# A gated delta rule laid out anew in a three-block kernel, with head norms and expert one-hots in other forms

## What is computed

```python
decay = exp(where(incl, gc[:, None] - gc[None, :], -inf))        # gc: running sum of g in the chunk
kk = einsum('id,jd->ij', k * beta, k) * decay
a_mat = eye + where(strict, kk, 0)
u, w = solve(a_mat, v * beta), solve(a_mat, k * beta * exp(gc))
attn = einsum('id,jd->ij', q, k) * decay
def step(state):                                                   # over the chunks
    v_new = u - w @ state
    o = (q * exp(gc)) @ state + attn @ v_new
    state = state * exp(g_last) + (k * exp(g_last - gc)).T @ v_new
```

## Time and profile before

| | us |
|---|---|
| median of 3 runs | 4513.59 |
| lowest and highest | 4506.96, 4524.67 |
| the profiled execution | 4514.63 |
| its span in the profile | 4512.9 |

### The profile page before, as it was taken

One profiled execution on the slowest core, in us unless ns is written; L12 is line 12 of the kernel. 1 busy time (PEld: TensorE's weight loads), 2 busy tenths in 40 slices (PEclk: granted clock), 3 DMA queues, 4 the chain that ended last, 5 costly groups with the idle time before them and its releaser, 6 DMA issues. The chain is left out here.

```text
span 4512.9 us, 50869 instructions
## 1 busy us (share of the span) xinstructions
PE 3787.8 (84%) x18835; PEld 3223.6 (71%) x18835; DVE 2688.0 (60%) x3850; ACT 1178.9 (26%) x1989; POOL 562.7 (12%) x381
## 2 busy tenths in 40 slices
PE   7998966799976556799899998999968877679998
PEld 6876753588755346579889898999946837556876
DVE  4444777444345565439999967777743447564433
ACT  1101123211031201113377773333321112322300
POOL 0000021000000020001456662222200000000000
PEclk9999978899988868899999999999979988889999
DMA  3222700222212000225888789999912102011232
GB/s 139 98 72 83 271 15 1 100 93 74 77 38 83 0 6 1 89 76 183 290 271 284 281 303 325 329 328 322 319 53 89 56 21 75 2 65 62 96 98 70
DMA packets 198406, 590.97 MB, mean 131 GB/s; under 512 B 22336, under 2 KB 80704, under 8 KB 196040
## 3 DMA queue, kind: packets, MB, share of 16 engines
q1 hardware_dynamic: 161368, 454.46, 29.2%
q0 software_dynamic: 36864, 134.23, 8.4%
HBM read 536.19 MB, written 52.43 MB: 130 GB/s over the span
## 5 line engine op out<-in xcount | busy, mean ns | idle before, releaser
L332 DVE CAST w_hi<-w_ring 128x1024 fp32r<-128x1024 f32 (+1 forms) x336 | 238.6, 710 | 642.4 <-PE banks L297 493.7
L71 DVE TENSOR_TENSOR w_lo<-w_ring,w_hi 128x1024 fp32r<-128x1024 f32 (+1 forms) x336 | 424.6, 1264 | 11.5
L297 PE MATMUL banks<-x_hi,w_hi 128*128 128x512 f32 x896 | 355.8, 397 | 48.2 <-DVE x_lo L71 47.4
L1803 PE MATMUL up_ps<-h_hi,u_hi 128*128 128x384 f32 x1024 | 358.5, 350 | 35.8 <-DVE u_lo L71 35.6
L2083 PE MATMUL out_ps<-w_hi,v_hi 128*128 128x384 f32 x1024 | 346.8, 339 | 42.3 <-DVE w_lo L71 42.3
L297 PE MATMUL banks<-x_lo,w_hi 128*128 128x512 f32 x896 | 354.1, 395 | 0.0
L297 PE MATMUL banks<-x_hi,w_lo 128*128 128x512 f32 x896 | 353.9, 395 | 0.0
L1803 PE MATMUL up_ps<-h_lo,u_hi 128*128 128x384 f32 x1024 | 349.3, 341 | 0.0
L1803 PE MATMUL up_ps<-h_hi,u_lo 128*128 128x384 f32 x1024 | 348.8, 341 | 0.0
L2083 PE MATMUL out_ps<-w_hi,v_lo 128*128 128x384 f32 x1024 | 345.4, 337 | 0.0
L2083 PE MATMUL out_ps<-w_lo,v_hi 128*128 128x384 f32 x1024 | 345.3, 337 | 0.0
(11 more groups left out here) (495 smaller groups left out, 8113.5 us busy)
## 6 DMA issues: line engine op xcount, KB each, us to landing
expert_tiles<-peer_u SPq DMA_DIRECT2D x128, 512.0 KB
expert_tiles<-peer_v SPq DMA_DIRECT2D x128, 512.0 KB
w_ring<-w_in SPq DMA_DIRECT2D x104, 512.0 KB, 3.7
w_ring<-ffn_up SPq DMA_DIRECT2D x88, 512.0 KB, 3.4
w_ring<-w_ff SPq DMA_DIRECT2D x64, 512.0 KB, 3.7
ada_ring<-w_ada SPq DMA_DIRECT2D x48, 512.0 KB, 5.4
peer_acts<-act_ring SPq DMA_DIRECT2D x128, 192.0 KB
peer_gates<-staging SPq DMA_DIRECT2D x12, 2048.0 KB, 11.1
```

The lines of the kernel that those rows point to most:

```text
L71: return nc.vector.tensor_tensor(self.lo[at], value, self.hi[at].bitcast(F32), ALU.subtract)
L297: last = nc.tensor.matmul(banks[:, j, s, 0:n], a[:, u % 2, k, :], b[:, g * kg + k, x_from + c:x_from + c + n], start=(g == 0 and k == 0 an ...
L332: nc.vector.tensor_copy(w_parts.hi[:, u % 2], ring[:, u % slots]).then_inc(hi_ready, 1)
L1803: last = nc.tensor.matmul(up_ps[:, n % 3, 0:DENSE], a[:, n % 2, k, :], b[:, k, P:T], start=(k == 0 and part_ == 0), stop=(k == DB - 1 and ...
```

## The change

1. **Head norms.** `head_norm` now uses `HeadColumns`: the sums of squares come from matmuls with the squares as weights and one column of ones (tokens on partitions, 4 per tile), so root and reciprocal act on 128x16 or 128x32; ScalarE then draws diagonals (128x128, 4 per tile) that TensorE spreads over all partitions, and VectorE reads them from PSUM. The norm in `hgrn_and_conv` uses `HeadRows`: sums of the 4 heads on 4 partitions, one root and one reciprocal of 4x512, spread by 4 matmuls with 4 weight rows.
2. **Step sizes.** `delta_steps` is one block in place of the projection of a and b, the tables, the norm of q and k, softplus, sums: a and b come out as 128x8 per chunk of tokens (32 matmuls of 8 columns), the softplus runs on 128x16, and the compensated sums stay on 4x512 rows, with the scaling of q and k between them.
3. **Distances.** `delta_products` forms a chunk's whole distance in one matmul of stacked high and low sums (`left`, `own`), ScalarE takes Relu and Exp, and v and k are turned in the same block. Nothing is loaded.
4. **Inverse.** `delta_inverse` sets the first level directly (a mask and a transpose), runs five levels in full and half of the last, and uses the waits for growing q and k.
5. **Chain.** `delta_chain` forms the part of the values that does not depend on the state, and the weights WT of the state, ahead; a chunk's step is then a product with the state added in PSUM, a copy by ScalarE (which scales by beta), and the state's update.
6. **Loads.** The tables of the block-2 mixer are fetched behind the first weight tiles of its first `linear`; the two `load` blocks there and the two in the delta rule are gone.
7. **Experts.** 96 candidates of 256 are kept per head, the two products of hits and indices move from GpSimd to VectorE, the first one-hot is one fused compare-and-multiply per token (4 of 128x128 per group in place of one 128x512 on each of two engines), GpSimd keeps only the gathers, and the table of costs and phases has other numbers (tiles 14, 9, 32, 27, 25, 19 in place of 16, 9, 27, 26, 26, 22).

ScalarE at the head of the delta rule, before: squares of q and k (`sq`), roots (`rstd`), the sigmoid of beta (`rows`), `small` the exponent of a_log, and the softplus' two steps.

All 8 products of hits and all 96 of gates have left its queue. The diff, cut to its core:

```diff
+class HeadColumns:
...
+    def sum(self, pe, b, square):
+        for c in range(NC):
+            last = self.p.nc.tensor.matmul(self.sums[:, b, c:c + 1], square[:, c * P:c * P + P], self.p.ones[:, 0:1],
+                                           start=True, stop=True)
+        last.then_inc(self.summed, 1)
...
+    def draw(self, act, b):
+        if b == 0:
+            act.wait_ge(self.inverted, 1)
+        if b >= 2:
+            act.wait_ge(self.spread, b - 1)
+        for c in range(NC):
+            last = self.p.nc.scalar.activation(self.diag[:, b % 2, c, :], self.p.ident, ACT.Copy, scale=self.cols[:, b, c:c + 1])
+        last.then_inc(self.drawn, 1)
+    def spread_to(self, pe, b, bank):
+        pe.wait_ge(self.drawn, b + 1)
+        for c in range(NC):
+            last = self.p.nc.tensor.matmul(bank[:, c * P:c * P + P], self.p.ones, self.diag[:, b % 2, c, :],
+                                           start=True, stop=True)
+        last.then_inc(self.spread, 1)
...
+class HeadRows:
...
+    def sum(self, pe, b, square):
...
+        self.p.nc.tensor.matmul(self.sums[:], self.strip[:, self.nb - 1 - b:2 * self.nb - 1 - b], square,
+                                start=(b == 0), stop=(b == self.nb - 1)).then_inc(self.summed, 1)
...
+    def spread_to(self, pe, b, bank):
+        pe.wait_ge(self.inverted, 1)
+        self.p.nc.tensor.matmul(bank, self.sel[:, b, :], self.root, start=True, stop=True).then_inc(self.spread, 1)
...
-                    nc.vector.reciprocal(rms[:, sl], rms[:, sl]).then_inc(normed, 1)
...
+                    dve.wait_ge(norm_rows.spread, h + 1)
...
-                nc.vector.reciprocal(rstd[:, g, :], rstd[:, g, :]).then_inc(inverted, 1)
...
+def delta_steps(p, h, w_ab, small, qkv, beta, left, right, head_mask, grown, decayed):
...
+            for b in range(NB):
+                pe.wait_ge(sq_ready, b + 1)
+                norm_.sum(pe, b, sq[:, b, :])
+            for b in range(NB):
+                if b == 1:
+                    pe.wait_ge(g_ready, 1)
+                    for c in range(NC):
+                        last = nc.tensor.transpose(row_ps[:, c * P:c * P + P], g[:, c, :], p.ident)
+                    last.then_inc(rows_turned, 1)
+                if b >= 4:
+                    pe.wait_ge(scaled, b - 3)
+                norm_.spread_to(pe, b, banks[:, b % 4, :])
...
+            scale(1)
+            dve.wait_ge(row_taken, 1)
...
+            then(nc.vector.tensor_tensor_scan(hi, keep[:], g_row[:], 0.0, ALU.mult, ALU.add))
...
+            scale(2)
...
+            scale(3)
+            then(nc.vector.tensor_tensor(err, hi, lo[:], ALU.subtract))
+            then(nc.vector.tensor_tensor(err, prev, err, ALU.subtract))
...
-                        nc.tensor.matmul(bank_a[:, h, :], sel[:, h, :], rows[:, 1, :], start=True, stop=True) \
-                            .then_inc(spread, 1)
...
+            def distance(j):
+                pe.wait_ge(own_ready, j + 1)
+                if j >= 2:
+                    pe.wait_ge(floored, j - 1)
+                for c in range(NC):
+                    last = nc.tensor.matmul(dist_ps[:, j % 2, c, :], left[:, at(c)], own[:, j % 2, at(c)], start=True, stop=True)
+                last.then_inc(dist_done, 1)
...
+                nc.scalar.activation(tile, dist_ps[:, j % 2], ACT.Relu, scale=-1.0).then_inc(floored, 1)
+                act.wait_ge(floored, j + 1)
+                nc.scalar.activation(tile, tile, ACT.Exp, scale=-1.0).then_inc(decay_ready, 1)
...
+def delta_inverse(p, masks, qkv, col, N, XT, k_rows, k_grown):
...
+            for l in range(1, LEVELS):
+                n = l - 1
+                pe.wait_ge(level_ready, l)
+                for j in range(H):
+                    pe.wait_ge(begun, 2 * H)
+                    if n:
+                        pe.wait_ge(updated, 2 * H * (n - 1) + 2 * j + 2)
+                    for c in range(NC):
+                        i = j * NC + c
+                        columns = slice(0, HALF) if l == LAST else slice(0, P)
+                        last = nc.tensor.matmul(bank_a[:, j, c, columns], N_l[:, l % 2, i, :], X[:, i, columns], start=True, stop=True)
+                    last.then_inc(y_ready, 1)
+                for j in range(H):
+                    pe.wait_ge(y_taken, H * n + j + 1)
+                    if n == 0:
+                        pe.wait_ge(q_grown, j + 1)
+                    for c in range(NC):
+                        i = j * NC + c
+                        if l == LAST:
+                            last = nc.tensor.matmul(bank_b[0:HALF, j, c, 0:HALF], Y[:, i, 0:HALF], XT[:, i, HALF:], start=True, stop=True)
+                            continue
+                        nc.tensor.matmul(bank_b[:, j, c, :], Y[:, i, :], XT[:, i, :], start=True, stop=True)
+                        last = nc.tensor.matmul(bank_a[:, j, c, :], XT[:, i, :], Y[:, i, :], start=True, stop=True)
+                    last.then_inc(z_ready, 1)
...
+def delta_chain(p, qkv, beta, through, attn, v_rows, k_rows, k_grown, XT, o):
...
+            def outputs(c):
+                pe.wait_ge(w_taken, NC - 1)
+                if c >= 2:
+                    pe.wait_ge(o_taken, c - 1)
...
+                for j in range(H):
+                    bank = o_ps[:, c % 2, j, :]
+                    last = nc.tensor.matmul(bank, vn[:, c % 2, j, :], attn[:, j * NC + c, :], start=True, stop=(c == 0))
+                    if c:
+                        last = nc.tensor.matmul(bank, S[:, (c - 1) % 2, j, :], q[:, j, c * P:c * P + P], start=False, stop=True)
...
+            own_values(0)
+            state_weights(1)
+            carry(0)
+            own_values(1)
+            state_weights(2)
+            values(1)
+            state_weights(3)
+            outputs(0)
+            carry(1)
+            values(2)
+            outputs(1)
+            carry(2)
+            values(3)
+            outputs(2)
+            outputs(3)
...
-    MIDDLE = [2.6] + [0.85] * 4 + [1.0] * 8 + [0.85] * 4 + [1.0] * 4 + [3.9]
-    COSTS = {"route": HEAD + MIDDLE + [4.6, 2.3, 1.1], "gate": [0.72] * GROUPS, "dot": [1.3] * SLOTS}
+    MIDDLE = [1.8] + [0.5] * 4 + [0.65] * 8 + [0.5] * 4 + [0.65] * 4 + [4.2]
+    COSTS = {"route": HEAD + MIDDLE + [2.3, 4.6, 2.3, 2.3, 1.1], "gate": [1.15] * GROUPS, "dot": [1.3] * SLOTS}
...
-            def hits(c, j):
-                pool.wait_ge(hit_made, 2 * c + j + 1)
-                i2 = idx_f[:].rearrange("p (h two) k -> p h two k", two=2)
...
-            def weights(g):
-                c, at = g // GROUPS + 1, g % GROUPS * GROUP_TOKENS
-                pool.wait_ge(row_ready, g + 1)
-                nc.gpsimd.tensor_tensor(gated[:, g % HOTS], gated[:, g % HOTS],
-                                        over(picks[:, c % 2, 2, at:at + GROUP_TOKENS].unsqueeze(2), [P, GROUP_TOKENS, NKEYS]),
-                                        ALU.mult).then_inc(weights_ready, 1)
...
+                for at, first, rows, width in ((0, 0, 2, K), (32, 2, 2, 8), (48, 4, 12, 4)):
+                    shape = [P, H, rows, width]
+                    then(nc.vector.tensor_tensor(
+                        cand[:, :, at:at + rows * width].rearrange("p h (a b) -> p h a b", a=rows),
+                        over(v2[:, :, 0, first:first + rows].unsqueeze(3), shape),
+                        over(v2[:, :, 1, 0:width].unsqueeze(2), shape), ALU.add))
...
+                i2 = idx_f[:].rearrange("p (h two) k -> p h two k", two=2)[:, :, 1, :]
+                flat = hit[:].rearrange("p h k a -> p (h k) a")
+                for j, (marks, relation, table) in enumerate(((row_start[:], ALU.is_ge, row_diff[:]), (iota[:, 0:K], ALU.is_equal, i2))):
+                    then(nc.vector.tensor_tensor(flat, over(part_f[:, j].rearrange("p h k -> p (h k)").unsqueeze(2), [P, H * K, K]),
+                                                 over(marks.unsqueeze(1), [P, H * K, K]), relation))
                     yield
...
+                    settled()
+                    then(nc.vector.tensor_tensor(hit[:], hit[:], over(table.unsqueeze(2), [P, H, K, K]), ALU.mult))
+                    yield
+                    settled()
+                    then(nc.vector.tensor_reduce(token[:, j, :], flat, AX.X, ALU.add))
...
-                nc.vector.tensor_tensor(gated[:, g % HOTS], over(iota[:].unsqueeze(1), shape),
-                                        over(picks[:, c % 2, 0, at:at + GROUP_TOKENS].unsqueeze(2), shape), ALU.is_equal) \
-                    .then_inc(row_ready, 1)
+                for t in range(at, at + GROUP_TOKENS):
+                    nc.vector.tensor_scalar(gated[:, g % HOTS, t - at, :], iota[:], picks[:, c % 2, 0, t:t + 1],
+                                            picks[:, c % 2, 2, t:t + 1], ALU.is_equal, ALU.mult).then_inc(weights_ready, 1)
...
-        head_norm(p, o, dst, gain, o, H, 1, out=dst)
+        head_norm(p, o, dst, gain, dst, H)
```

1097 lines of the change are left out of this document (613 added, 484 removed).

## The result

| | before | after |
|---|---|---|
| median, us | 4517.24 (4 runs) | 4333.45 (4 runs) |
| lowest and highest | 4506.96, 4524.67 | 4323.88, 4340.69 |
| span of the profiled execution | 4512.9 | 4338.9 |

The ratio is 0.9593, with a 95% interval from 0.9566 to 0.9621: 184 us less, where 189 were forecast. The profiled execution after is the slowest of its four; its span is 174.0 us shorter than the one before.

What follows compares the result with a forecast made beforehand. Bounds: a serial delta-rule stage (294 us) whose engines mostly wait for one another, and the experts' first half, with at most 64 us to give. Terms 118 + 7 + 15 + 7 + 42 = 189 off 4514.6 give 4325, range 4275 to 4390.

Steps and rivals of the forecast that it cites:

- Steps: Delta rule's first block, from z through the scaling of q and k: 44 us against 86.4, bounds 36 and 50.
- Products: Delta rule's products of k, distances and turns: 80 at 0.21 us plus start and copies, 23 us against 46.
- Inverse: Delta rule's inverse: 8.5 us of VectorE start, five levels of 10.7, half level 6.5; 69 us against 90.
- Chain: Delta rule's four chunks, with part of the values formed ahead: 23 us against 47, bounds 19 and 34.
- Norm: Norm at the delta rule's end, behind the chunks: 17 us against 23, bounds 14 and 19.
- block 1: Block 1's norm: three of four reciprocals go, four-row products come; 7 us less, bounds 4 to 10.
- retention: Retention's norm, 44 us with 27 in reciprocals: 15 us less, bounds 10 to 20.
- Experts: Experts' first half, 692 us: lifting GpSimd's hold on VectorE and evening the phases gives 42 us less, bounds 0 and 60.
- A, the clock stays low: Delta rule: narrow products and idle gaps keep TensorE's clock low; 35 us less gain, retention 5; time 4365, chance 0.17.
- B, the experts' half gives nothing: Experts' first half: fused operations hold up GpSimd's gathers, VectorE waits for rows; the 42 us vanish, 4367, chance 0.15.
- C, the floor: Experts' first half reaches TensorE's floor, another 18 to 22 us, and delta-rule lower bounds 11 more: 4292, chance 0.2.
- D: Kernel slower: the experts' fused operation costs far more than its nearest row, 0.74 us each undoing 189 us; chance 0.02.

## Why the prediction was right, and where it was not

The time (4333 against 4325) and the signs of all terms were right. By its own steps:

- **What bounds.** The three views were enough: the reading that the first part and the chain count steps, the inverse counts matmuls, and that the experts' half can give no more than 64 us held. It gave 51, by the mean of eight profiles.
- **Steps, 44 forecast, 46.6 measured.** The 64 products ahead of the root took 10.6 + 13.8 = 24.4 us against 22; the forecast that narrow products lower the clock was right, at 0.67 and then 0.50. The widening shows that it was the width here: with 128 columns in both places the clock stayed at 1.00. The prediction took that from the earlier trace rows without proof.
- **Products, 23 forecast, 18.6 measured.** Mis-sized on the safe side, and in the turns. The start at half clock did take place: TensorE had no work for 6.37 us before the block, then ran at 0.50 for 4.1 us and at 0.87 for 4 more, at the price of some 2.5 us (an estimate: those two stretches at 1.00 would have taken 2.0 and 3.5), where I had put 3. But I had put the 32 turns at 0.21 us each, the price of a product. A turn stands as one record and takes half of that, 0.11 us (the group behind the eight of the last row begins 0.87 us after them), 3.5 us in all in place of 6.7; the statement ahead of the prediction that a plain f32 matmul has two rows doesn't hold for them. TensorE's first group, and then 8 records each (4 products, 8 turns) at nearly full clock:

```profile
1552.09 2.05 PE L1446 MATMUL kk_ps<-qkv 128*128 128x128 f32 x8 [6.37 <-PEq L1270]
1559.00 1.06 PE L1451 MATMUL qk_ps<-qkv 128*128 128x128 f32 x8
1559.89 1.04 PE L1467 MATMUL turn_ps<-consts,qkv 128*128 128x128 f32 x8
```

- **Inverse, 69 forecast, 74.5 measured.** This is the step that failed. The prediction let "GpSimd's mask of 4.5 us, released a level ahead," stay hidden. Its first one starts with the block and holds VectorE's first four operations up, which stand on the path; 6.85 us in place of the 2.8 that I counted, so that the first full level began 12.9 us into the block and not 8.5. TensorE also started at 0.50 there (1576 to 1580), behind 5.94 us without work. The growing of q and k, for which I named VectorE's idle time as cover, was held up in the same way (8.46 us for three); beside it the first two full levels took 11.0 and 11.7 us in place of 10.7, and "a level over 11" was one of the signs that I had named. The mechanism stood in my own text, for the experts' half. I priced it there and forgot it here.
- **Chain, 23 forecast, 21.5 measured**, at a clock of 1.00. The step in which `outputs(1)` delays `carry(2)` was read rightly from the order, but what I took for a cost can't be had back by a swap.
- **Norm, 17 forecast, 19.0 measured; block 1, 7 and 5.0; retention, 15 and 11.9.** All three too hopeful by 2 or 3 us. In the delta rule's norm the sums began 2.1 us in and took 6.0 at a clock of 0.59, so they ended at 8.2 where I had 6.5, and the spreading ran at 0.73. In retention the sums begin 2.3 us into the stage and take 13.8 at half clock, so the root comes at 16.2 us where I had 14, and the first tile at 20.4 where I had 17, with the drawing and spreading ahead of it.
- **Loads, 7 forecast, 7.9 measured.**
- **Experts, 42 forecast, 47.3 measured here, 51 by the mean.** The three parts were right: L71's mean is 1.22 us against 1.49, VectorE's sum 578 against the 568 that I worked out, and the half 645 to 641 against 650. The two runs that put GpSimd's products back cost 16 us each. If the two add up, the lifting of its hold is 32 of the 51 us, the larger part, and the shorter lists have the rest; no run has both at once, nor the shorter lists by themselves, so this split is argued and not shown. The price of the fused operation, put at 0.22 to 0.29, was 0.30: the nearest row had one column as scalar, and the second costs 0.08.
- **What I had at nothing.** The second half was 8.6 us longer in this profile. It is chance: the same code took 569.7 in the kernel with only the experts' part. Together with 3.3 in other stages it is the reason why this execution shows 174 us and not the 186 that the terms sum to; the medians differ by 184.
- **How much was luck.** The delta rule came to 180 where 176 were forecast, but as a sum of errors that cancel: products 4.4 and chain 1.5 better, steps 2.6, inverse 5.5 and norm 2.0 worse. That the total is right to 9 us of 4333 says less than the list does.

**Rivals.** *A, the clock stays low:* its premise was half right. Narrow products put it at half, and gaps did so too: 0.50 behind 6.37 us without work at the start of the products, and 0.50 behind 5.94 at the start of the inverse, which cost an estimated 2 to 2.5 us each (half of the 4 us that each stretch at 0.50 lasted, and a little at 0.87 behind the first). But it did not stay there; it was back at 1.00 in the later spreading products, on the row from 1538.2 above, and in the whole chain. *B, the experts' half gives nothing:* VectorE's wait for gathered rows rose from 20 to 34 us, beyond the 20 that I had named as a sign against me, and yet the half gave all of it. The sign was badly chosen. It measures how early VectorE comes, not how late the rows are; without gathers the half is only 10 us shorter. The Trainium skill's rule on this, on the page SBUF — State Buffer, section Who interferes with whom, speaks of GpSimd and such one-source operations locking each other out; the trace can't tell their hold from other causes, but all that gathers cost here, by whatever way, is those 10 us, and in the fourth phase, where the fused operations run beside gathers, taking the gathers away changed nothing (140.3 us both). *C, the floor:* the half came within 15 to 20 us of TensorE's 626. *D* had the operation at 0.74 us and it was 0.30.

## What to carry to other kernels

Count a GpSimd product as VectorE time wherever the two overlap, also at the head of a block where VectorE's first operations stand on the path: it isn't booked as a wait, it shows as a mean or a maximum far above the median of equal instructions. A product with one or a few columns took no less time here than one with 128 (21 records of 8 columns in 2.2 us at full clock, 0.105 us each, against 0.109 for the records of wide ones), and the clock fell under a row of them; widening them over columns that are thrown away gave about 20 us (11.3 in the delta rule, 6.2 in retention, 2.6 in block 1). And compare stages, not only medians: 3 us in a stage that repeats to 0.1 are plain to see, where the whole kernel's time varies by 10.
